# FFN operands ahead of additions, norms with two buffers, a new tile order for the group norm

## The reference, cut to what matters

```python
# first block, after the two branches
o_a = mla_branch(...)                    # attention, 512 wide
o_b = fwd + bwd                          # each: (head_group_norm(scan) + bonus) * gate
y_a = o_a @ w_o[:512]; y_b = o_b @ w_o[512:]
gates = sigmoid(gate_cols + b_gate)
x = x + (gates[0] * y_a + gates[1] * y_b) @ w_merge
h = rms_norm(x, norm_ffn_g)
gp = dwconv_centered(h @ w_ffn_gate, ffn_conv_w, ffn_conv_b)
x = x + (silu(gp) * (h @ w_ffn_up)) @ w_ffn_down
# second block: projections, gated linear attention and convolution, @ w_out, then
x = x + mixed
h2 = rmsnorm(x, norm2_g)
x = x + (silu(h2 @ w_ffn_gate) * (h2 @ w_ffn_up)) @ w_ffn_down
return rmsnorm(x, norm_f_g)
```

## Time and profile before

| | us |
|---|---|
| median of 3 runs (3656.99 to 3657.79) | 3657.28 |
| the profiled execution | 3656.53 |
| its span, first to last instruction | 3654.7 |

### The profile page before, as it was taken

One profiled execution on the slowest core, in us unless ns is written; L12 is line 12 of the kernel. 1 busy time (PEld: TensorE's weight loads), 2 busy tenths in 40 slices (PEclk: granted clock), 3 DMA queues, 4 the chain that ended last, 5 costly groups with the idle time before them and its releaser, 6 DMA issues.

```text
span 3654.7 us, 61041 instructions
## 1 busy us (share of the span) xinstructions
PE 3431.7 (94%) x27176; PEld 2721.4 (74%) x27176; DVE 1718.2 (47%) x2528; ACT 1107.7 (30%) x1789; POOL 323.9 (9%) x342
## 2 busy tenths in 40 slices
PE   8999998999999987999999999899899899999998
PEld 7678676777777873477887888677677688878876
DVE  4453555665556557454335434542454522352235
ACT  4323324444444320132123222332332311231124
POOL 1232241111111212000000000001000000000000
PEclk9999999999999999999999999999899999999999
DMA  3241252211111204321112211222002111121112
GB/s 137 70 142 47 81 181 80 71 43 51 37 57 45 98 23 150 123 81 41 52 46 93 70 47 52 98 100 94 24 29 104 58 52 47 62 89 63 46 70 98
DMA packets 89974, 269.82 MB, mean 74 GB/s; under 512 B 11552, under 2 KB 12080, under 8 KB 89712
## 3 DMA queue, kind: packets, MB, share of 16 engines
q1 hardware_dynamic: 78960, 230.26, 18.5%
q0 software_dynamic: 10752, 35.66, 2.9%
HBM read 219.73 MB, written 46.14 MB: 73 GB/s over the span
## 4 chain that ended last, share of the span: by engine, by line
PE 82%; DVE 11%; ACT 3%; issue 2%; DMA 1%; SPq 0%; POOL 0%; DVEq 0%; ACTq 0%
PE ps L355 77%; PE ps L354 3%; DVE X L364 3%; PE ps L358 2%; DVE SM L375 2%; DVE AR L364 1%; DVE OTB L364 1%; ACT HT L1144 1%; DVE HT L368 1%; DVE HL L364 1%; DVE W L364 1%; ACT HH L361 1%; ACT W L2017 0%; DVE EX L364 0%; ACT WS L361 0%
## 5 line engine op out<-in xcount | busy, mean ns | idle before, releaser
L355 PE MATMUL ps<-HH,WS 128*128 128x512 f32 (+1 forms) x3232 | 1001.2, 391 | 0.0
L355 PEld LDWEIGHTS ps<-HH,WS 128*128 128x128 f32 (+1 forms) x3232 | 607.7, 188 | 129.4
L355 PE MATMUL ps<-HL,WS 128*128 128x512 f32 x1616 | 639.4, 396 | 10.3 <-DVE HL L364 10.1
L364 DVE TENSOR_TENSOR WS<-W,WS 128x1024 fp32r<-128x1024 f32 (+1 forms) x245 | 300.1, 1225 | 640.1 <-ACT WS L361 639.6
L355 PE MATMUL ps<-WS,SA 128*128 128x512 f32 x2112 | 494.6, 395 | 42.4 <-DVE SA L364 42.4
L361 ACT ACTIVATE WS<-W 128x1024 fp32r<-128x1024 f32 (+1 forms) x245 | 257.6, 1051 | 906.3 <-PE ps L355 894.4
L355 PEld LDWEIGHTS ps<-WS,SA 128*128 128x128 f32 x2112 | 400.3, 191 | 133.8 <-DVE SA L364 29.7
L355 PEld LDWEIGHTS ps<-HL,WS 128*128 128x128 f32 x1616 | 304.0, 188 | 76.4 <-issue 10.7
L355 PE MATMUL ps<-WS,HL 128*128 128x512 f32 x576 | 210.1, 399 | 13.1 <-DVE WS L364 8.5
L355 PE MATMUL ps<-WS,HH 128*128 128x512 f32 x640 | 205.8, 398 | 14.6 <-DVE HL L364 6.0
L355 PE MATMUL ps<-HL,HI 128*128 128x512 f32 (+1 forms) x512 | 209.0, 408 | 3.7 <-POOL WL L364 2.8
(11 more groups left out here) (280 smaller groups left out, 4402.0 us busy)
## 6 DMA issues: line engine op xcount, KB each, us to landing
W<-in_w_fd SPq DMA_DIRECT2D x88, 512.0 KB, 3.2
AR<-rw_d SPq DMA_DIRECT2D x104, 256.0 KB, 4.0
W<-in_w_fg SPq DMA_DIRECT2D x44, 512.0 KB, 3.2
W<-in_w_fu SPq DMA_DIRECT2D x44, 512.0 KB, 3.2
W<-in_w_tok SPq DMA_DIRECT2D x24, 512.0 KB, 3.3
rw_d<-X POOLq DMA_DIRECT2D x40, 256.0 KB, 3.2
X<-in_x SPq DMA_DIRECT2D x16, 512.0 KB, 10.0
W<-in_w_g SPq DMA_DIRECT2D x16, 512.0 KB, 3.6
```

The costliest lines, as they stand in the source:

```text
L355: return pe.e.matmul(o, l, r, start=start, stop=stop)
L364: return e.e.tensor_tensor(o, x, y, op)
```

## The change

1. `lora` in `prep_pe` waits for "ul" 13 in place of 15.
2. Group norm: token tiles in the order 3, 4, 2, 5, 1, 6, 0, 7; the wait for all of the scans' stores (`dma_o`) is split off and is made only by SP ahead of tiles 7 and 0 and of the W loads, and by ACT; PE has no wait here at all. Two buffers for the bonus. The output moves from OBT3 to four pieces in EX and AR, so ACT copies each tile in two. PE and DVE make three steps of `outa` ahead of the interleaving, not two.
3. `outb`: the x reloads go between the gate loads; the first weight gets a place of its own (WFIRST), is loaded ahead of `outb`'s gates and split in `outb`'s second half; weights 1 to 4 are loaded as W's tiles are read.
4. Norms: two buffers (OTB and a piece of SM); the low half of one buffer is made after the multiplication into the other.
5. `tok_pe` and `down_pe` take each bank right ahead of its first matmul, not four at once.
6. `down_steps`: the low (and high) half 0 of the next group is made ahead of a group's additions, half 1 after the second of them.

```diff
@@ prep_pe
-                    pe.wait_ge(*at("ae_rw", "ul", 15))
+                    pe.wait_ge(*at("ae_rw", "ul", 13))
@@ places
-        SQT = AR[:, 6144:10240]
-        OBT3 = v3(AR[:, 10240:14336], 4)
+        SQT = AR[:, 6144:8192]
+        BON, ACC = [SQT[:, 0:512], SQT[:, 1536:2048]], [SQT[:, 512:1024], SQT[:, 1024:1536]]
+        OBT = [EX[:, 2048:3072], EX[:, 3072:4096], AR[:, 12288:13312], AR[:, 13312:14336]]
+        TORD = (3, 4, 2, 5, 1, 6, 0, 7)
+        WFIRST = AR[:, 14336:15360]
@@ gn_sp
-            scans_over(sp)
-            for t in range(NT):
+            scans_done(sp)
+            for n_, t in enumerate(TORD):
+                if t in (0, 7):
+                    stored(sp, int(t == 0))
                 for d in range(2):
                     sp.e.dma_start(OF[d][:, t * 512:(t + 1) * 512], o_d[d, t]).then_inc(*dma(f"dma_of{t}", d))
                 sp.e.dma_start(VV[:, t * 512:(t + 1) * 512], rw_d[t, 2]).then_inc(*dma(f"dma_of{t}", "all"))
-                if t == 3:
+                if n_ == 3:
+                    stored(sp, 1)
@@ gn_ve
-                    if t >= 2:
-                        ve.wait_ge(*at("pe_mix", "gT", t - 2))
+                    if n >= 2:
+                        ve.wait_ge(*at("pe_mix", "gT", TORD[n - 2]))
@@ gn_ge
-                if t:
-                    ge.wait_ge(*at("ve_mix", "acc", t - 1))
+                if n >= 2:
+                    ge.wait_ge(*at("ve_mix", "acc", TORD[n - 2]))
@@ outb_sp
-            for t in range(NT):
-                sp.e.dma_start(xt(t), a["x"][t * P:(t + 1) * P, :]).then_inc(*dma(f"dma_x{t}", "again"))
+            sp.e.dma_start(WFIRST, todo[0][0]).then_inc(*dma("dma_wfirst", 0))
...
                     sp.e.dma_start(GT[n % 4], g_d[8 + n, h]).then_inc(*dma(f"dma_gt{n % 4}", "b", h, n))
+                    if h == 0:
+                        sp.e.dma_start(xt(n), a["x"][n * P:(n + 1) * P, :]).then_inc(*dma(f"dma_x{n}", "again"))
@@ outb_ve, outb_ae
+                    if h and n == 4:
+                        sp.one()
@@ weights_sp
+                if 1 <= i < 5:
+                    sp.wait_ge(*at("pe_mix", "b", 1, 2 * i - 1))
                 load_w(sp, todo[i][0], "split", i, n=todo[i][1])
@@ norm_ve
+            def rest(t, h):
+                hi, lo = [z[:, 4 * h:4 * h + 4, t * P:(t + 1) * P] for z in (HH3, HL3)]
+                ve.wait_ge(*at("ae_" + nm, "hi", t, h))
+                tt(ve, lo, NTT[h], hi.bitcast(F32), ALU.subtract).then_inc(*ve.sig("ve_" + nm, "lo", t, h))
...
                 ve.wait_ge(*at("pe_" + nm, t, h))
-                tt(ve, NTT, v3(ps[:, bank(nm, t, h), :], 4), bl(gain[:, 4 * h:4 * h + 4], P),
+                tt(ve, NTT[h], v3(ps[:, bank(nm, t, h), :], 4), bl(gain[:, 4 * h:4 * h + 4], P),
                    ALU.mult).then_inc(*ve.sig("ve_" + nm, "t", t, h, frees=(nm, t, h)))
-                ve.wait_ge(*at("ae_" + nm, "hi", t, h))
-                tt(ve, lo, NTT, hi.bitcast(F32), ALU.subtract).then_inc(*ve.sig("ve_" + nm, "lo", t, h))
+                if h:
+                    rest(t, 0)
+                elif t % 4:
+                    rest(t - 1, 1)
+                if h and t % 4 == 3:
+                    rest(t, 1)
@@ tok_pe (down_pe alike)
-                    bs = [take(pe, nm, tg * 4 + j, nh, banks=MAIN) for j in range(4)]
+                    bs = []
...
                             for j in range(4):
+                                if k == 0:
+                                    bs.append(take(pe, nm, tg * 4 + j, nh, banks=MAIN))
@@ down_steps
+            for g in range(4):
+                tg, nh = divmod(g, 2)
+                for q in range(nf // 2):
+                    sp.take()
+                    for kk in range(2):
+                        if g == 0 or q:
                             part(tg, nh, 2 * q + kk)
+                    sp.one()
+                    bk.step()
+                    bk.step()
+                if g < 3:
+                    part(*divmod(g + 1, 2), 0)
+                for j in range(4):
+                    evac(tg * 4 + j, nh)
+                    if g < 3 and j == 1:
+                        part(*divmod(g + 1, 2), 1)
@@ tensor_program (vector_program alike, with its own scans_done)
-            scans_over(pe)
-            next(outa)
-            next(outa)
+            for _ in range(3):
+                next(outa)
             interleave(outa, gn_pe(pe))
@@ sync_program
             outb_sp(sp)
-            mix_over(sp)
             plan.fresh(RING)
-            weights_sp(sp, 0, first["tok2"] + 4)
+            weights_sp(sp, 1, first["tok2"] + 4)
```

More of the change, by code:

```diff
@@ L1769, in gn_pe @@
         def gn_pe(pe):
-            for t in range(NT):
+            for n, t in enumerate(TORD):
                 for d in range(2):
@@ L1784, in gn_ve @@
             ve.wait_ge(*at("ve_mix", "var"))
-            for t in range(NT):
-                bon = SQT[:, 0:512]
-                acc = SQT[:, 512 + 512 * (t % 2):1024 + 512 * (t % 2)]
+            for n, t in enumerate(TORD):
+                bon, acc = BON[n % 2], ACC[n % 2]
                 for d in range(2):
@@ L1839, in outb_sp @@
         def outb_sp(sp):
-            sp.wait_ge(*at("ve_mix", "acc", NT - 1))
-            sp.wait_ge(*at("ae_mix", "gT", NT - 1))
-            for t in range(NT):
-                sp.e.dma_start(xt(t), a["x"][t * P:(t + 1) * P, :]).then_inc(*dma(f"dma_x{t}", "again"))
+            sp.wait_ge(*at("ve_mix", "acc", TORD[-1]))
+            sp.wait_ge(*at("ae_mix", "gT", TORD[-1]))
+            sp.e.dma_start(WFIRST, todo[0][0]).then_inc(*dma("dma_wfirst", 0))
             for h in range(2):
@@ L1964, in one @@
                 ve.wait_ge(*at("ae_split", i))
-                tt(ve, wlo(i), wtile("split", i)[:, 0:todo[i][1]], whi(i).bitcast(F32), ALU.subtract).then_inc(
-                    *ve.sig("ve_split", i, frees=("w", "split", i)))
+                tt(ve, wlo(i), whole(i), whi(i).bitcast(F32), ALU.subtract).then_inc(
+                    *ve.sig("ve_split", i, frees=("w", "split", i) if i else None))
             return Split(one)
@@ L2158, in down_pe @@
                 for nh in range(2):
-                    bs = [take(pe, nm + "d", f0, tg * 4 + j, nh, banks=MAIN) for j in range(4)]
+                    bs = []
                     for q in range(nf // 2):
@@ L2169, in down_pe @@
                             for j in range(4):
+                                if k == 0:
+                                    bs.append(take(pe, nm + "d", f0, tg * 4 + j, nh, banks=MAIN))
                                 o = ps[:, bs[j], :]
@@ L2189, in down_steps @@
         def down_steps(sp, bk, nf, part, evac):
-            for tg in range(2):
-                for nh in range(2):
-                    for q in range(nf // 2):
-                        sp.take()
-                        for kk in range(2):
-                            part(tg, nh, 2 * q + kk)
-                        sp.one()
-                        bk.step()
-                        bk.step()
-                    for j in range(4):
-                        evac(tg * 4 + j, nh)
+            for g in range(4):
[4 more added lines that the diff above has]
+                        if g == 0 or q:
+                            part(tg, nh, 2 * q + kk)
+                    sp.one()
+                    bk.step()
[6 more added lines that the diff above has]
+                        part(*divmod(g + 1, 2), 1)
         def before_sa(f0, nf, tg, nh, k):
@@ L2787, in vector_program @@
             scans(ve, scan_ve, att_ve, outa)
-            scans_over(ve)
+            scans_done(ve)
             var_ve(ve)
-            next(outa)
-            next(outa)
+            for _ in range(3):
+                next(outa)
             interleave(outa, gn_ve(ve))
-            outb_ve(ve)
+            outb_ve(ve, sp)
             bk.start(norm_ve(ve, "nf", pc["g_ffn"], mix_over))
@@ L2846, in gpsimd_program @@
             scans(ge, scan_ge, att_ge, nothing())
[L2847 removed]
+            scans_done(ge)
             gn_ge(ge)
```

53 lines of the change are left out of this document (28 added, 25 removed).

## The result

The changed kernel takes 3592.9 us (median of 4 runs, 3591.1 to 3595.7), the kernel before 3657.5 in the same comparison: ratio 0.982, 95% interval 0.981 to 0.984, so it is 1.8% faster. Forecast were 3600, with 3585 to 3625 as the range. The profiled execution has a span of 3591.4, 63.4 less than before.

The account below looks back on a forecast made before the run. TensorE was taken to bound the kernel: its work, its gaps and low clock after gaps. Terms 11.8 - 3.3 + 9.7 + 10.8 + 7.0 + 14.5 + 4.2 + 2.7 = 57.4 off 3656.5 gave 3599.1, with 0.75 3600; range 3585 to 3625.

Parts of the forecast that it names:

- E: First FFN matmuls of the second half, twice: two norm buffers shorten the 5.05 us wait; gain 3.5 each, 7.0.
- F: Joins of the down products: next group's low half made earlier, banks free; nine plain joins 13.3, in all 14.5 gained.
- G: Norm n1 inside the second down product: four stalls lose 0.1 each, group's end 2.58 to 0.3, clock 1.5; gain 4.2.
- C: From `outb` to merge: first weight loaded and split early, so TensorE's 8.53 us idle time goes; gain 9.7.
- D: Merge and w_out, group 3 to 4: two 4.5 us waits for evacuations shrink, with less low clock; together 10.8 gained.
- A: Lora wait before prep: TensorE's 7.63 us idle time and low clock go, carried through the stage; gain 11.8.
- B: Scans to group norm: all norm tiles fall behind a queued gate load, norm ends 6.8 later; net loss 3.3.
- rival (3): Prep does not carry the lora gain on, because GpSimd's low halves or stores bind; 3612 us, chance 4%.
- Rival (4): Slower: low clock after TensorE's idle time in the group norm holds to `outb`'s end; 92 lost, 3692 us, 3%.
- H: tok2, group 1 to 2: the 3.44 us wait behind ACT's copies becomes 0.75; gain 2.7.
- Rival (2): Joins find a next wait, weight's split or ACT's order: F, D and E shrink, 21 us lost, 3621; chance 15%.
- Rival (5): The clock swings at each join of the down products: 12 times 1.7 us more gained, 3580 us; chance 1%.

## Why the prediction was right, step by step

The sum of gains was 57.4 and the profile's is 63.4. Of the 6.0 missed, E holds 2.0, F and G 2.0, the way to w_out 1.8, C and D 0.6 each; A and B took 0.6 each away. (The rest of the 7.1 between 3600 and 3592.9 is medians against profiled executions.)

**A** held (11.2 of 11.8), its clock term included. The matmuls ahead of `lora(0)` ended at 423.1 before and at 423.6 after; from there to the decay matmuls the gain is 11.7, and undone it is 11.6. Prep carried it: rival (3) is out, as far as one profile of each can say, since prep's own length differs by up to 4.6 between kernels.

**B** held in mechanism and size. SP's first load went 4.16 us after `outa`'s start, DVE stood 19.2 us until the gate load, and all of the norm lay behind. The norm's end came 7.3 later (6.8 forecast), less the `outa` unit: 3.9 lost. TensorE's earlier start was worth nothing. The 0.5 more are DVE waiting for TensorE at half clock in the first tiles, which no step had:

```profile
1398.04 0.69 DVE L364 TENSOR_TENSOR AR<-HT,ps 128x512 f32<-128x512 f32 x1 [0.59 <-PE ps L355]
```

Rival (4) is out: between 1395 and 1444 the clock was low only for short times, and from 1444 on it is 1.00.

**C** was low by 0.6: no bank was late, and a stop more was saved.

**D** held: 11.4 of 10.8, and the runs split it as forecast between banks (2.2 each, 2.1 forecast) and second buffer. Beside it 1.8 us came around w_out's start that no step had: the wait there fell from 6.00 to 5.44 and the half clock behind it lasted 10 matmuls less.

```profile
2788.70:2796.00 7.30, 7.28 (x20) 5.76 (x21) 3.25 (x2) 0.00 (x0) 0.00 (x0) 0.58 0.80 313
2796.00:2805.00 9.00, 9.00 (x41) 7.46 (x40) 2.31 (x2) 2.12 (x2) 0.00 (x0) 1.00 0.17 60
```

```profile
2747.00:2751.00 4.00, 3.84 (x10) 3.09 (x11) 3.94 (x4) 0.58 (x1) 0.00 (x0) 0.58 1.02 415
2751.00:2760.00 9.00, 9.00 (x41) 7.43 (x40) 1.22 (x1) 1.14 (x2) 0.00 (x0) 1.00 0.48 168
```

(w_out's start before, then after). With banks taken at once the wait was 5.99 again, with the buffer or the down products put back it stayed 5.44. That points to the banks for the 0.56; by what path is open. The half clock behind it is mostly luck: in seven of the other eleven kernels whose wait is 5.44 it lasted longer again.

**E** had the idle time right and the clock wrong. In the second half's norm TensorE's stops of 0.3 us and more add up to 9.6 us before and 6.0 after, in both FFNs: 3.6 less, for 3.5 forecast. But the forecast wanted the last stop to stay at about 5 us, and the low clock behind it with it. It fell to 3.47, and the low level lasted 6.8 us in place of 10.2. That is the 2.0 missed in both together. FFN 1 and 2 after, to be held against 0.53 in the fifth window of the earlier trace rows:

```profile
1624.00:1635.00 11.00, 6.86 (x23) 5.20 (x22) 4.81 (x8) 2.21 (x4) 0.00 (x0) 0.69 0.01 1
2856.00:2867.00 11.00, 6.45 (x21) 4.94 (x22) 5.52 (x9) 2.52 (x4) 0.00 (x0) 0.69 0.00 0
```

With one buffer it lasted 10.2 us again. The sign "gaps of 5, clock low behind" failed in its number.

**F and G** together gave 20.7 of 18.7. The nine plain joins are the mis-sized term. Each was priced at the idle time shown, 1.48 us, and is worth 1.73 (5.18 and 5.21 for three, and 5.20 and 5.28 lost when undone). The 0.25 between are in the rows. A matmul is drawn 0.39 us long but follows its neighbour at 0.227, so the idle time before the next one is counted from 0.16 too late; and the first matmul behind a stop takes 0.31 to its follower, 0.08 more (the next two 0.01). For the nine plain joins that is 2.2 us. The fourth product gave 0.5 more beside them, 0.2 of it in a stop of 1.63 near its start that is now 1.39. The second, with G, fell short by 0.9 of its other terms. What failed there is G's clock term: 1.5 us of it were forecast, and the low level lasted 20.5 us in this product before and after.

The Trainium skill, "TensorE: Matmul & The Clock Gate", section "Single matmul latency", gives (398 + N)/2.4 ns for one bf16 matmul at the higher level, 379 ns for N = 512; its section "Step-by-step: what each phase is for" says that in a stream the drain of one overlaps the fill of the next. The 0.39 and 0.227 us here are near that, for fp32r. But the profile models where a matmul ends, so 0.39 is no measurement of its own; what is measured are the starts. From the last start ahead of a join to the next it is 1.864 us. Less the 0.227 of an even stream, and with the 0.09 behind it, that is the 1.73.

**H** held: 2.8 of 2.7, with 0.62 us of its 3.44 left (0.75 forecast).

**Rival (2)**, a next wait at the joins, did not come: the weight's split (DVE 1.22 us) still fits, and eleven joins show no stop. **Rival (5)** is out by its own test: taking away the 1.48 us stops gained 0.25 each beyond their idle time and not 1.7.

## What to carry to other kernels

Price a stop of TensorE at the idle time shown plus 0.25 us (shown here for stops of 1.48 us between 512-column matmuls), and look at the clock behind it apart. When a wait is moved ahead in an in-order queue, list what then stands behind it: here the third step of `outa` cost 4.6 us and the freed start gave 4.0, and moving three pairs of gate loads up the queue returned 15.8 us. At a join make the next operand before freeing what the next group does not yet need; count the banks in the ring before deciding which addition it waits for.

## What the runs showed of the hardware

**Stops of TensorE and the clock.** The joins of 1.48 us did not lower the clock, nor did six stops of 0.4 to 0.7 in 32 us (the window at 1.00 above). The Trainium skill, "TensorE: Matmul & The Clock Gate", section "A second HAM failure mode: psum-queue depth-cycling", tells of micro-idle times between groups that make the clock swing; this case has them at a pitch of 4 us and shows no swing. Stops of 2.2 to 3 us may lower it or not. Each down product begins behind one of 2.21 to 2.33 us, 56 times in the 14 kernels; in 45 the clock stayed at 1.00 there and in 11 it fell. The start of the first down product behind a stop of 2.26 us, in the changed kernel and in the one with one buffer:

```profile
1884.00:1893.00 9.00, 8.71 (x38) 7.24 (x39) 4.58 (x6) 3.34 (x5) 0.00 (x0) 1.00 0.17 58
```

```profile
1894.00:1903.00 9.00, 8.50 (x30) 6.85 (x31) 3.32 (x5) 2.84 (x5) 0.00 (x0) 0.81 0.17 58
```

The product took 130.94 us in the one and 132.58 in the other. And in one kernel (banks at once) the windows behind a stop of 2.94 us and behind one of 2.88 us read

```profile
1586.90:1591.00 4.10, 4.06 (x20) 3.44 (x21) 2.66 (x4) 0.00 (x0) 0.00 (x0) 1.00 0.25 52
2825.20:2829.00 3.80, 3.78 (x11) 3.04 (x12) 2.10 (x3) 0.00 (x0) 0.00 (x0) 0.63 0.19 49
```

Where four such stops follow each other, the same code took between 132.6 and 137.2 us in eight kernels that leave the second down product alone, with the same stops (3.4, 3.3, 3.4, 2.85) to 0.1 us; the clock in the 46 us window was 0.85 in the shortest and 0.79 in the changed kernel. So a single profile gives such a stretch to about 2 us either way only.

**DVE beside GpSimd.** Of the two stretched operations of a tile, in the changed kernel, GpSimd's and DVE's rows:

```profile
1389.23 1.04 POOL L364 TENSOR_TENSOR AR<-AR,SM 128x512 f32<-128x512 f32 x1 [23.12 <-DVE AR L364]
1390.36 1.59 POOL L364 TENSOR_TENSOR AR<-AR,W 128x512 f32<-128x512 f32 x1
```

```profile
1389.61 1.22 DVE L364 TENSOR_TENSOR X<-X,SM 128x512 f32<-128x512 f32 x1
1390.86 1.64 DVE L364 TENSOR_TENSOR X<-X,W 128x512 f32<-128x512 f32 x1
```

GpSimd ends at 1390.27 and 1391.95, DVE 0.56 and 0.55 later. The even distance says that DVE did not run slower but stood until GpSimd was through (an operation alone takes it 0.69). GpSimd pays as well: its second operation takes 1.26 us while DVE waits for the gate load (start 1364.85) and 1.59 here, where it starts while DVE's first is under way. The Trainium skill, "SBUF — State Buffer", section "Who interferes with whom", states this as an exclusive lock between a DVE operation with two inputs in SBUF and a GpSimd operation that reads SBUF; the rows agree. It is about the 1.4 us by which a tile with a bonus beside it is longer.
